# Experts in the order of their blocks: weights loaded once per expert and addressed by a register, row transfers issued by ScalarE

## What is computed

```python
gl = ht @ w_group_router + group_bias            # 4 groups; the best one is taken
el = ht @ w_expert_router + expert_bias          # 4 experts in each group
e_val, e_loc = lax.top_k(softmax(el of the group), 2)
gates = group_prob * e_val / sum(e_val)          # two of 16 experts for each token
a = einsum('td,edf->tef', ht, w_e_gate)          # 1024 -> 256
u = einsum('td,edf->tef', ht, w_e_up)            # 1024 -> 256
out = (silu(a) * u * gates) @ w_e_down           # 256 -> 1024, summed over the two experts
```

## Time and profile before

| | us |
|---|---|
| median of 3 runs | 2456.46 |
| lowest and highest | 2452.45, 2467.61 |
| the profiled execution | 2461.02 |
| its span in the trace | 2459.2 |
| PE busy | 2143.7 (87%) |
| DVE busy | 1251.4 (51%) |
| ACT busy | 848.6 (35%) |

### The profile page before, as it was taken

One profiled execution on the slowest core, in us unless ns is written; L12 is line 12 of the kernel. 1 busy time (PEld: TensorE's weight loads), 2 busy tenths in 40 slices (PEclk: granted clock), 3 DMA queues, 4 the chain that ended last, 5 costly groups with the idle time before them and its releaser, 6 DMA issues. The chain is left out here.

```text
span 2459.2 us, 30224 instructions
## 1 busy us (share of the span) xinstructions
PE 2143.7 (87%) x11466; PEld 1810.9 (74%) x11466; DVE 1251.4 (51%) x2347; ACT 848.6 (35%) x1381; POOL 501.6 (20%) x343
## 2 busy tenths in 40 slices
PE   6988897899999698989889999969799998378884
PEld 6888676788888688867678888859777878266763
DVE  3675544444443367544444444369602242468775
ACT  3443332322220344333242222133214451266662
POOL 2653310000000265331000000033513343200001
PEclk9999988999999799888899999979859999589997
DMA  3111101322210211110132221048812121389995
GB/s 134 60 45 35 35 1 52 137 103 102 102 68 0 91 66 39 35 35 1 47 142 103 103 101 70 0 146 181 204 47 74 60 103 35 149 319 359 356 354 217
DMA packets 60623, 265.11 MB, mean 108 GB/s; under 512 B 15568, under 2 KB 20304, under 8 KB 36048
## 3 DMA queue, kind: packets, MB, share of 16 engines
q1 hardware_dynamic: 58192, 255.03, 29.7%
q0 software_dynamic: 2304, 8.39, 0.9%
HBM read 240.36 MB, written 35.09 MB: 112 GB/s over the span
## 5 line engine op out<-in xcount | busy, mean ns | idle before, releaser
L415 PE MATMUL ffn_up<-f_hi,ffn_gu_hi 128*128 128x512 f32 x704 | 276.3, 392 | 15.1 <-DVE ffn_gu_lo L386 12.3
L415 PE MATMUL ffn_up<-f_lo,ffn_gu_hi 128*128 128x512 f32 x704 | 275.6, 392 | 0.0
L415 PE MATMUL ffn_up<-f_hi,ffn_gu_lo 128*128 128x512 f32 x704 | 275.4, 391 | 0.0
L1028 PE MATMUL fill_ps<-mix_whi,h_hi 128*128 128x256 f32 (+1 forms) x704 | 213.9, 304 | 15.3 <-DVE mix_wlo L914 8.3
L1028 PE MATMUL fill_ps<-mix_whi,h_lo 128*128 128x256 f32 (+1 forms) x704 | 204.6, 291 | 0.0
L1028 PE MATMUL fill_ps<-mix_wlo,h_hi 128*128 128x256 f32 (+1 forms) x704 | 204.1, 290 | 0.0
L369 DVE TENSOR_TENSOR ffn_silu<-ffn_silu,ffn_up 128x512 f32<-128x512 f32 x44 | 30.2, 687 | 293.5 <-ACT ffn_silu L341 293.5
L415 PEld LDWEIGHTS ffn_up<-f_hi,ffn_gu_hi 128*128 128x128 f32 x704 | 133.1, 189 | 44.3 <-DVE ffn_gu_lo L386 12.9
L1488 POOL TENSOR_TENSOR w_lo<-two_raw,w_hi 128x1024 fp32r<-128x1024 f32 x48 | 122.6, 2570 | 196.4 <-ACT w_hi L1576 196.4
L1028 PEld LDWEIGHTS fill_ps<-mix_whi,h_hi 128*128 128x128 f32 x704 | 141.0, 200 | 28.7 <-DVE mix_wlo L914 9.1
L381 DVE TENSOR_TENSOR x<-ffn_down,x 128x512 f32<-128x512 f32 x176 | 119.6, 689 | 80.6 <-PE ffn_down L430 79.8
(11 more groups left out here) (422 smaller groups left out, 5218.3 us busy)
## 6 DMA issues: line engine op xcount, KB each, us to landing
moe_raw_gu<-in_w_e_gu SPq DMA_DIRECT2D x46, 1024.0 KB, 12.9
mix_raw<-in_w_mix SPq DMA_DIRECT2D x30, 1024.0 KB, 4.9
two_raw<-in_w_two SPq DMA_DIRECT2D x25, 1024.0 KB, 5.2
moe_raw_d<-in_w_e_down SPq DMA_DIRECT2D x23, 1024.0 KB, 8.8
ffn_raw_gu<-in_w_gate SPq DMA_DIRECT2D x22, 1024.0 KB, 5.0
ffn_raw_gu<-in_w_up SPq DMA_DIRECT2D x22, 1024.0 KB, 6.2
ffn_raw_d<-in_w_down SPq DMA_DIRECT2D x22, 1024.0 KB, 4.8
moe_in<-in_zero SPq DMA_DIRECT2D x23, 512.0 KB, 18.3
```

What stands on the lines that cost most here:

```text
L415: last = nc.tensor.matmul(up_ps[m][b][:], ww[:, m, k, b * P:(b + 1) * P], aw[:, k, :], start=n == 0, stop=n == 3 * KD - 1)
L1028: last = nc.tensor.matmul(b[:, 0:cols], aw[:, k, t * P:(t + 1) * P], ww[:, k, 0:cols], start=k == 0 and n == 0, stop=k == KD - 1 and n == 2)
```

## The change

- `route` places an expert's blocks one behind the other, in the order of the experts: expert e starts at block (blocks of the experts before it). It writes a `plan` of 78 integers instead of `spill_of`: for each block the number of experts begun (which is its expert plus one) and the buffer (the expert's parity), for each expert the number of blocks done when it is through, once and doubled (for the halves).
- SP loads each expert's weights once, 16 times 3 MB in place of 23. It reads from `plan` how many blocks must have been split before a buffer is free. It also waits for each expert's weights to land and passes that on in two semaphores, `gu_ready` (both halves) and `d_ready`.
- ACT and DVE read from `plan` which buffer a block uses (ACT two values and DVE one for each block, `value_load`), and address the raw weights by that register. ACT waits for `gu_ready` and `d_ready` in place of the loads' own semaphores.
- ACT issues the row loads (for block b+2 right behind `x_turned` of b, ahead of `x_hi`) and the stores of the results (of b-2, behind `w_hi(b+1, 0)`).

The diff, cut to its core:

```diff
@@ route, dve @@
-                tt(spill, upto, more, ALU.subtract)
-                link(nc.vector.scalar_tensor_tensor(spill, spill, 1.0 * P, const[:, C_SPILL:C_SPILL + EXPERTS], ALU.mult, ALU.add))
-                upto_here = before_ps[:].rearrange("p (t e) -> p t e", t=TB)
-                own, spilled = place[:, 0], place[:, 1]
-                shape = [P, TB, EXPERTS]
-                link(nc.vector.scalar_tensor_tensor(spilled, upto_here, P + 0.5, bcast(spill.unsqueeze(1), shape), ALU.is_gt, ALU.mult))
-                tt(own, upto_here, bcast(const[:, C_OWN:C_OWN + EXPERTS].unsqueeze(1), shape), ALU.add)
-                tt(own, own, spilled, ALU.add)
+                tt(first, upto, more, ALU.subtract)
+                base = more
+                link(nc.vector.scalar_tensor_tensor(base, first, 1.0 * P, const[:, C_OWN:C_OWN + EXPERTS], ALU.mult, ALU.add))
+                own = place[:, 0]
+                tt(own, before_ps[:].rearrange("p (t e) -> p t e", t=TB), bcast(base.unsqueeze(1), [P, TB, EXPERTS]), ALU.add)
...
-                shape = [1, SPILLS, EXPERTS]
-                tt(spill_f[:], bcast(upto[0:1].unsqueeze(1), shape), bcast(const[0:1, C_COUNT:C_COUNT + SPILLS].unsqueeze(2), shape), ALU.is_le)
-                link(nc.vector.tensor_reduce(spill_n[:], spill_f[:], AX, ALU.add))
-                link(nc.vector.tensor_scalar(spill_of[:], spill_n[:], EXPERTS - 1.0, None, ALU.min))
...
+                expert = const[0:1, C_EXPERT:C_EXPERT + EXPERTS]
+                tt(first[0:1], first[0:1], expert, ALU.add)
+                tt(upto[0:1], upto[0:1], expert, ALU.add)
+                shape = [1, BLOCKS, EXPERTS]
+                tt(grid_f[:], bcast(first[0:1].unsqueeze(1), shape), bcast(const[0:1, C_COUNT:C_COUNT + BLOCKS].unsqueeze(2), shape), ALU.is_le)
+                link(nc.vector.tensor_reduce(plan_f[:, PLAN_UPTO:PLAN_UPTO + BLOCKS], grid_f[:], AX, ALU.add))
+                tt(grid_f[:], grid_f[:], bcast(const[0:1, C_SIGN:C_SIGN + EXPERTS].unsqueeze(1), shape), ALU.mult)
+                link(nc.vector.tensor_reduce(plan_f[:, PLAN_PLACE:PLAN_PLACE + BLOCKS], grid_f[:], AX, ALU.add))
+                link(nc.vector.tensor_scalar(plan_f[:, PLAN_PLACE:PLAN_PLACE + BLOCKS], plan_f[:, PLAN_PLACE:PLAN_PLACE + BLOCKS],
+                                             -1.0, 1.0, ALU.mult, ALU.add))
+                link(nc.vector.tensor_scalar(plan_f[:, PLAN_DONE:PLAN_DONE + EXPERTS], upto[0:1], 1.0, 1.0, ALU.mult, ALU.add))
+                link(nc.vector.tensor_scalar(plan_f[:, PLAN_HALVES:PLAN_HALVES + EXPERTS], upto[0:1], 2.0, 2.0, ALU.mult, ALU.add))
+                link(nc.vector.tensor_copy(plan[:], plan_f[:]))
@@ experts, sync @@
-                spills = [sp.value_load(spill_of[0:1, j:j + 1], min_val=0, max_val=EXPERTS - 1) for j in range(SPILLS)]
-                sp.wait_ge(scattered, 16 * CHOSEN * TB)
-                for b in range(BLOCKS):
-                    s = b % 2
-                    e = b if b < EXPERTS else spills[b - EXPERTS]
-                    if b >= 2:
-                        sp.wait_ge(x_turned, b - 1)
-                    sp.dma_start(xb[s], core.moe_in[b * P:(b + 1) * P, :]).then_inc(x_in[s], 16)
-                    if b >= 2:
-                        for h in range(2):
-                            sp.wait_ge(gu_lo_done, 2 * (b - 2) + h + 1)
-                            w_moe.load_gu(sp, e, s, h)
-                        sp.wait_ge(d_lo_done, b - 1)
-                        w_moe.load_down(sp, e, s)
-                    if b >= 4:
-                        store_y(b - 4)
...
+                def gu_there(e):
+                    for h in range(2):
+                        sp.wait_ge(gu_in[e % 2][h], 16 * (e // 2 + 1))
+                    sp.sem_inc(gu_ready, 1)
+
+                def down_there(e):
+                    sp.wait_ge(d_in[e % 2], 16 * (e // 2 + 1))
+                    sp.sem_inc(d_ready, 1)
+
+                for e in range(EXPERTS):
+                    if e >= 2:
+                        n = PLAN_HALVES + e - 2
+                        gu_used = sp.value_load(plan[0:1, n:n + 1], min_val=2, max_val=2 * BLOCKS)
+                        n = PLAN_DONE + e - 2
+                        d_used = sp.value_load(plan[0:1, n:n + 1], min_val=1, max_val=BLOCKS)
+                    if e >= 2:
+                        gu_there(e - 1)
+                        sp.wait_ge(gu_lo_done, gu_used)
+                        for h in range(2):
+                            w_moe.load_gu(sp, e, e % 2, h)
+                        down_there(e - 1)
+                        sp.wait_ge(d_lo_done, d_used)
+                        w_moe.load_down(sp, e, e % 2)
+                    if e == 0:
+                        gu_there(0)
+                        down_there(0)
...
@@ experts, scalar @@
                 def x_hi(b):
                     s = b % 2
                     act.wait_ge(x_turned, b + 1)
+                    if b + 2 < BLOCKS:
+                        load_x(b + 2)
...
                 def w_hi(b, h):
                     s = b % 2
-                    act.wait_ge(gu_in[s][h], 16 * (b // 2 + 1))
+                    if h == 0:
+                        upto[b], place[b] = of_block(act, b)
+                        act.wait_ge(gu_ready, upto[b])
...
                         x_hi(b + 1)
                         w_hi(b + 1, 0)
+                    if b >= 2:
+                        store_y(b - 2)
@@ experts, vector @@
                 def w_lo(b, h):
                     s = b % 2
+                    if h == 0:
+                        place[b] = place_of(dve, b)
```

More of the change, by code:

```diff
@@ L69 @@
 SLOTS = BLOCKS * P
+PLAN_UPTO, PLAN_PLACE, PLAN_DONE, PLAN_HALVES = 0, BLOCKS, 2 * BLOCKS, 2 * BLOCKS + EXPERTS
+PLAN = PLAN_HALVES + EXPERTS
 C_ID, C_TRI, C_ONE, C_CHUNK, C_CAUSAL = 0, P, 2 * P, 3 * P, 4 * P
@@ L77 @@
 C_OWN = C_RANK + 4
-C_SPILL = C_OWN + 16
-C_COUNT = C_SPILL + 16
-C_COLS = C_COUNT + 8
+C_EXPERT = C_OWN + 16
+C_SIGN = C_EXPERT + 16
+C_COUNT = C_SIGN + 16
+C_COLS = C_COUNT + 24
 PARAMS = (("fox_qn", HEAD), ("fox_kn", HEAD), ("diff_qn", DIFF_D), ("diff_kn", DIFF_D),
@@ L2232, in __init__ @@
         self.w = w
-        self.gu = [core.sb(f"moe_raw_gu{s}", [P, KD, 2 * HID], ctx=ctx) for s in range(2)]
-        self.down = [core.sb(f"moe_raw_d{s}", [P, HB, D], ctx=ctx) for s in range(2)]
+        self.gu = core.sb("moe_raw_gu", [P, 2, KD, 2 * HID], ctx=ctx)
+        self.down = core.sb("moe_raw_d", [P, 2, HB, D], ctx=ctx)
         self.gu_in = [[core.sem(f"moe_gu_in{s}{h}", ctx) for h in range(2)] for s in range(2)]
@@ L2251, in ahead, with route @@
             self.load_down(sp, s, s)
-def route(core, w, hi, lo, share, slot, spill_of):
+def route(core, w, hi, lo, share, slot, plan):
     nc = core.nc
@@ L2388, in _ @@
                 dve.wait_ge(counted, 1)
-                more, upto, spill = (extra[:, n] for n in range(3))
+                more, upto, first = (extra[:, n] for n in range(3))
                 link(nc.vector.tensor_scalar(more, count_ps[:], 1.0 * P, None, ALU.is_gt))
@@ L2457, in experts, with place_of, of_block, raw_gu @@
         y_out = [core.sem(f"moe_y_out{s}", st) for s in range(2)]
+        gu_ready, d_ready = core.sem("moe_gu_ready", st), core.sem("moe_d_ready", st)
         ident = core.const[:, C_ID:C_ID + P]
         gu_in, d_in = w_moe.gu_in, w_moe.down_in
+        def place_of(engine, b):
+            n = PLAN_PLACE + b
+            return engine.value_load(plan[0:1, n:n + 1], min_val=0, max_val=1)
+        def of_block(engine, b):
+            n = PLAN_UPTO + b
+            return engine.value_load(plan[0:1, n:n + 1], min_val=1, max_val=EXPERTS), place_of(engine, b)
+        def raw_gu(place, h):
+            return w_moe.gu[:, bass.ds(place, 1), h * HK:(h + 1) * HK, :].rearrange("p s k n -> p (s k) n")
+        def raw_down(place):
+            return w_moe.down[:, bass.ds(place, 1)].rearrange("p s k n -> p (s k) n")
         with nc.Block() as block:
@@ L2496, in _ @@
+                gu_there(EXPERTS - 1)
+                down_there(EXPERTS - 1)
                 for s in range(2):
@@ L2500, in _, with load_x, store_y @@
             def _(act):
+                def load_x(b):
+                    s = b % 2
+                    act.dma_start(xb[s], core.moe_in[b * P:(b + 1) * P, :]).then_inc(x_in[s], 16)
+                def store_y(b):
+                    s = b % 2
+                    act.wait_ge(y_act, b + 1)
+                    act.wait_ge(y_dve, b + 1)
+                    act.dma_start(core.moe_out[b * P:(b + 1) * P, :], y[s]).then_inc(y_out[s], 16)
+                upto, place = {}, {}
                 def x_hi(b):
@@ L2515, in w_hi @@
                     nc.scalar.copy(gu_hi[s][:, h * HK:(h + 1) * HK, :],
-                                   w_moe.gu[s][:, h * HK:(h + 1) * HK, :]).then_inc(gu_hi_done, 1)
+                                   raw_gu(place[b], h)).then_inc(gu_hi_done, 1)
                 def h_hi(b):
@@ L2526, in down_hi @@
```

(16 more changed lines are left out.)

26 lines of the change are left out of this document (10 added, 16 removed).

## The result

The kernel got slightly slower, against a forecast of 16 us less. Median after: 2470.68 us (2464.57 to 2479.31, 20 runs); of before, run beside it: 2462.48 (2452.26 to 2472.26, 20 runs). The ratio is 1.0037, interval 1.0023 to 1.0052, some 8 us.

The account below looks back on a forecast made before the run. Bound: a loop over two blocks, 11.8 us a block, through `down_lo`, DMA burst and weight landing. Terms: -14.2 (seven loads) -5.3 (11 blocks) +2.2 (`route`) +0.4 +0.9 (ACT) = -16.0 us, median 2456.5 to 2440.5; range 2430 to 2462.

Parts of the forecast that it names:

- Seven loads fewer: Last 7 blocks, `w_hi(15, 0)` to `w_hi(22, 0)`: without loads 11.78 falls to 9.75 us a block, 14.2 us gained.
- The floor: Compute pace in `experts` with DVE and PE nearly always busy: 9.55 us a block.
- a value near the floor: Last 7 blocks: 9.75 us a block, taking ACT's and DVE's register reads as mostly hidden.
- The bound of 10.9: Last 7 blocks: slowest pace, us a block, if no register read or DMA issue is hidden.
- The 11 blocks: `w_hi(4, 0)` to `w_hi(15, 0)`, still loading 3 MB each: 11.78 to 11.3 us a block, 5.3 us gained.
- (b): 11 blocks: `w_hi(b, 0)` waits for both halves of the gate and up weights, 1.2 us a block slower alone.
- (a): 11 blocks: rows and results leave SP's queue, taking 0.5 MB, 1.2 us, out of the burst.
- (c): 11 blocks: SP asks for the next 2 MB only after the last landed; half the slow start gone gives 11.3 us a block.
- slow start: Start of each DMA burst: down weights take 8.6 us from issue against 4.9 in the first bursts, 3.7 more.
- the wait for both halves decides: Rival, 11 blocks: that wait slows the pace to 12.0 to 12.9 us a block, 2448 to 2458.1 us; chance 0.2.
- a second issuer is worth nothing: Rival, 11 blocks: DMAs share the same engines, pace 11.6 to 12.0 us a block, 2444 to 2448 us; chance 0.15.
- (L + 0.2 + 9.4) / 2: 11 blocks: pace of the two-block loop, L from `down_lo` to the weights' landing; L of 13.0 gives 11.3 us.

Follow-up runs that it names:

- b_noload: The kernel before with the loads of blocks 16 to 22 left out and nothing else changed; 2445.21 us, ratio 0.9928 to before.
- b_actrows: The kernel before with row loads and result stores issued by ACT, all 23 weight loads still by SP; 2447.79 us, ratio 0.9941 to before.
- b_actrows_both: The kernel before with rows and results issued by ACT, and `w_hi(b, 0)` waiting for both halves; 2472.94 us, ratio 1.0047 to before.
- a_poolrelay: The changed kernel with the waits for landed weights and the posts of `gu_ready` and `d_ready` moved from SP to POOL; 2474.06 us, ratio 1.0047 to before.
- a_scatterfirst: The changed kernel with SP again waiting for the scatter to land before loading expert 2's weights; 2468.88 us, ratio 1.0041 to before.
- a_all: The changed kernel with all repairs: halves, POOL, scatter wait, early reads, rows behind `x_hi`, `store_y(21)` behind `h_hi(22)`; 2442.03 us, ratio 0.9899 to before.
- b_actrows_behind: The kernel before, ACT issuing rows (behind `x_hi`) and results, no loads for blocks 16 to 22, `store_y(21)` behind `h_hi(22)`; 2441.06 us, ratio 0.9911 to before.

## Why the prediction was wrong

The forecast was -16.0 us, the profiles give +7.5. The 23.5 us between lie at the following places. Beside them, the forecast stood on a median of before from three runs, 2456.5; twenty runs give 2462.5, and these 6 us are in the distance from 2440.5 to 2470.7 as well. With them added the range would end at 2468, and the time would still lie outside.

*Seven loads fewer*: right in kind, 3.1 us too much. The floor was right (9.53 in b_noload), and the DMA share there, 0.29, is below the 0.4 named as a sign. The step that failed is 9.75, "a value near the floor", for reads and an issue that were taken to be hidden because "DVE waits for ACT there anyway". That DVE waits for ACT is why they do cost: ACT is on the loop. They cost 0.30 and 0.36 us a block. The bound of 10.9 was on the safe side; 10.20 lies between.

*The 11 blocks*: 6.1 us too much. Its steps (11.78 to 12.9, 12.25 and 11.3) beside the runs, in us a block:

| step | forecast | measured | by |
|---|---|---|---|
| (b) wait for both halves | +1.1 | +1.27 | b_actrows to b_actrows_both, 10.41 to 11.68 |
| (a) rows and results leave SP's queue | -0.6 | -1.37 | before to b_actrows, 11.78 to 10.41 |
| (c) half of the slow start gone | -0.95 | +0.17 | b_actrows_both to after, 11.68 to 11.85 |

The step that failed is (c): it took away half of a slow start of 3.7 us, as a middle between two bounds, and no row showed that. In a_poolrelay SP doesn't wait for a landing before it asks for more, so (c) is not there at all, and the pace is the same (11.86 against 11.85). (a) was sized too small, which hid the larger part of this. The rival "the wait for both halves decides" had the mechanism, though 11.85 lies just below its 12.0. By its number the result falls to the rival "a second issuer is worth nothing" (11.6 to 12.0), and that is chance: alone the second issuer was worth more than 1 us a block.

The formula (L + 0.2 + 9.4) / 2 holds; what was wrong in it is L. Means over the weights of experts 5 to 14, from the issues and landings in the traces (us):

| | before | b_actrows_both | after | forecast |
|---|---|---|---|---|
| issue of the down weights to that of the gate and up weights | 1.36 | 0.37 | 2.30 | |
| from there to the landing of the second half | 14.9 | 13.8 | 11.8 | |
| L, both together | 16.2 | 14.2 | 14.1 | 13.0 |
| second half behind the first | 2.46 | 3.03 | 2.74 | 2.4 |
| pace by the formula | | 11.9 | 11.9 | 11.3 |
| pace measured | 11.78 | 11.68 | 11.85 | |

So L fell by 2.1, not by 3.1, and all of it came with (a): in b_actrows_both nothing holds SP up, and L is the same as after the change. The rows have left SP's queue but not the engines: they take 6.4 us there in the changed kernel against 3.3 in the last 7 blocks, where no weights flow. In the changed kernel SP's two reads and its wait for the landings make the weights leave 2.30 us behind the down weights (1.47 in a_poolrelay, with the reads alone), and they land the sooner for it (11.8 us, and 12.6 in a_poolrelay). L is 14.1 in both, and that is why POOL in SP's place moved nothing. With the halves apart POOL ran at 10.89 and SP at 11.13, which one profile each can't tell from chance.

*The start*, from the first scatter to `w_hi(4, 0)`: 12.4 us, of which 0.4 were forecast. The forecast has no term for SP's wait for `scattered`, which the change takes away: I did not ask what transfer is set free and what it meets. It is 5.4 us of slower scatters. From `x_turn(0)` to `w_hi(4, 0)` come 7.1 more. The same stretch in the other kernels divides them:

| | us | more than the one above |
|---|---|---|
| before | 34.2 | |
| b_actrows | 35.7 | 1.5, rows and results issued by ACT |
| b_actrows_both | 38.1 | 2.4, the wait for both halves |
| a_poolrelay | 40.3 | 2.2, open |
| after | 41.3 | 1.0, SP's count |

SP's count for expert 2 comes behind `down_lo(0)`, though its weights had landed by 2168.3:

```profile
2158.67 0.81 SPq L2244 DMA_DIRECT2D moe_raw_gu<-in_w_e_gu  x2
2193.09 0.33 SPq L2248 DMA_DIRECT2D moe_raw_d<-in_w_e_down  x1
```

`w_hi(2, 0)` runs at 2194.72. With POOL it comes 2.3 us sooner behind `x_turn(0)`, of which 1.0 is left at `w_hi(4, 0)`. The scatter's 5.4 us don't show in the whole time of a_scatterfirst: 1.0041 and 1.0037, with intervals of 0.0020 and 0.0015 to each side, where 5.4 us is 0.0022. The profiles show them, and they are not given back later: from the first scatter to `w_hi(4, 0)` it is 60.8 us against 66.2, to `w_hi(22, 0)` 260.4 against 267.9.

*The end of `route`*: +2.2 forecast, +2.2 measured. The four operations of 368 columns took 0.52 to 0.53 each, 0.50 estimated.

*The end*: 0.9 forecast for `store_y(21)`, 2.6 measured, and 0.6 behind it, which is no more than scatter: over the 14 kernels that stretch takes 30.6 to 31.9. The same order gives 22.0 to 23.7 over ten kernels; with `h_hi(22)` ahead (a_all, b_actrows_behind) it is 21.1, as before. So it costs 0.9 to 2.6.

Of the chances, within 1% (0.78) is what came. The range ended at 2462 because each of its cases moved one term and left the others at their forecast. Here the 11 blocks, the last 7, the start and the end all missed in the same direction, and the start, the largest miss, had no case at all.

## What to carry to other kernels

When one semaphore stands for several transfers, the first consumer pays for the last of them: here 1.27 us a block, 14 us over the 11 blocks, where leaving out seven loads saved 11. Moving small transfers to an engine that computes is worth it where they stood behind large ones, but each issue and each register read then belongs behind the operation that the loop runs through, not ahead of it. And where a change takes a wait from a queue, cost the transfer that starts early by what it meets.

## What the runs showed of the hardware

- Rows issued by ACT land while SP's weights are under way: 7.6 us in place of 10.2, with 1.0 to 1.4 us a block gained. The Trainium skill's page named above has each engine go round between the queues (section "Queues, rings and completion order"); these landings agree with that. In the traces the two sets of transfers go by queues q1 and q10.
- Two loads of 1 MB among eight indirect scatters took these from 4.2 to 9.5 us from issue to landing; with the loads held back until the scatters had landed it was 4.0.
- The reads of registers on ACT and DVE are short (the load itself 0.27 us on ACT), and still cost 0.30 us a block where they stand ahead of a cast on the loop. A DMA issue there holds ACT's queue for 0.33 us and costs 0.36 us a block.
